# Softmax probabilities normalised ahead of the transposes instead of after the value product

## The reference, cut to what matters

```
N_HEADS = 8; SEQ = 512; CTX_LEN = 256; QK_NOPE_DIM = 64; QK_ROPE_DIM = 32; V_HEAD_DIM = 64
def mla_attend(q_nope, q_rope, k_nope, k_rope, v):
    scale = (QK_NOPE_DIM + QK_ROPE_DIM) ** -0.5
    s = (jnp.einsum('bqhd,bkhd->bhqk', q_nope, k_nope)
         + jnp.einsum('bqhr,bkr->bhqk', q_rope, k_rope))
    pr = jax.nn.softmax(s.astype(jnp.float32) * scale, axis=-1).astype(v.dtype)
    return jnp.einsum('bhqk,bkhd->bqhd', pr, v)
```

## Time and profile before

| what | value |
|---|---|
| median of 3 runs | 885.34 us (885.32 to 887.03) |
| profiled execution, span | 883.6 us |
| busy share over the span: PE, DVE, ACT, POOL | 94 %, 51 %, 43 %, 43 % |
| attention stage, first scores to the end of the last row factors | 138.14 to 246.04 us of the span, 107.9 us |
| busy in that stage: PE, DVE, ACT, POOL | 97.1, 84.0, 75.7, 45.1 us |

### The profile page before, as it was taken

How to read it: one execution, slowest core, us unless ns; L and a number is a source line. 1 busy time by engine, 2 the same in 40 slices (tenths; PEclk the granted TensorE clock), 3 DMA queues, 4 the chain that set the end, 5 groups by cost and what they waited for, 6 DMA issues and landing times.

```text
span 883.6 us, 11658 instructions
## 1 busy us (share of the span) xinstructions
PE 828.0 (94%) x3976; PEld 680.0 (77%) x3976; DVE 451.6 (51%) x560; ACT 376.4 (43%) x580; POOL 376.2 (43%) x191
## 2 busy tenths in 40 slices
PE   5679968999899999999999899999999999999995
PEld 4458856888688888888858798888888888888884
DVE  5853797888723257666423566555555555100014
ACT  6763445778622323222234355444444444211134
POOL 0095352466235445746532335444444444444420
PEclk9979989999999999999999899999999999999998
DMA  8923210011032469856552214333333332322202
GB/s 291 331 64 70 67 48 1 1 48 26 25 90 73 147 194 282 253 176 194 165 166 72 72 29 139 97 97 100 100 100 99 95 95 95 96 96 95 71 1 95
DMA packets 126239, 96.22 MB, mean 109 GB/s; under 512 B 13468, under 2 KB 111033, under 8 KB 126201
## 3 DMA queue, kind: packets, MB, share of 16 engines
q1 hardware_dynamic: 126169, 95.71, 36.0%
q10 hardware_dynamic: 32, 0.01, 0.0%
HBM read 93.60 MB, written 2.10 MB: 108 GB/s over the span
## 4 chain that ended last, share of the span: by engine, by line
PE 77%; DVE 10%; issue 4%; ACT 3%; DMA 3%; POOL 1%; SPq 1%; ACTq 0%; DVEq 0%
PE ps L340 24%; PE ps L342 24%; PE ps L341 24%; DVE small L972 2%; POOL ht L488 1%; PE ps L1357 1%; DVE work L949 1%; DMA xt<-x_dram 1%; PE ps L1346 1%; PE ps L1437 1%; DVE work L953 1%; DVE klo L940 1%; DMA xt<-ctx_dram 1%; DMA raw<-w_in_dram 1%; SPq L223 1%
## 5 line engine op out<-in xcount | busy, mean ns | idle before, releaser
L279 POOL TENSOR_TENSOR wlo<-raw,whi 128x1024 fp32r<-128x1024 f32 (+2 forms) x131 | 306.2, 2342 | 392.2 <-ACT whi L271 391.7
L340 PE MATMUL ps<-hhi,whi 128*128 128x512 f32 (+1 forms) x648 | 251.1, 388 | 8.0 <-DVE hlo L889 4.8
L341 PE MATMUL ps<-hlo,whi 128*128 128x512 f32 (+1 forms) x648 | 249.2, 385 | 0.0
L342 PE MATMUL ps<-hhi,wlo 128*128 128x512 f32 (+1 forms) x648 | 248.9, 384 | 0.0
L271 ACT ACTIVATE whi<-raw 128x1024 fp32r<-128x1024 f32 (+2 forms) x148 | 144.6, 988 | 107.5 <-PE ps L342 88.7
L340 PEld LDWEIGHTS ps<-hhi,whi 128*128 128x128 f32 x648 | 123.5, 191 | 34.0 <-DVE hlo L889 4.8
L342 PEld LDWEIGHTS ps<-hhi,wlo 128*128 128x128 f32 x648 | 123.7, 191 | 23.7
L341 PEld LDWEIGHTS ps<-hlo,whi 128*128 128x128 f32 x648 | 123.7, 191 | 23.5 <-issue 0.5
L1154 DVE SCALAR_TENSOR_TENSOR work<-ps,prm,work 128x511 f32<-128x511 f32 x44 | 33.0, 749 | 76.8 <-ACT work L812 75.9
L1025 DVE SCALAR_TENSOR_TENSOR adacc<-ada,cvec,adacc 128x1024 f32<-128x1024 f32 x28 | 62.2, 2236 | 15.6 <-DMA ada<-w_ada_dram 15.5
L340 PE MATMUL ps<-fhi,whi 128*128 (+1 forms) x176 | 69.2, 393 | 0.1
(11 more groups left out here) (232 smaller groups left out, 1253.1 us busy)
## 6 DMA issues: line engine op xcount, KB each, us to landing
raw<-w_up_dram SPq DMA_DIRECT2D x88, 256.0 KB, 3.1
raw<-w_in_dram SPq DMA_DIRECT2D x66, 256.0 KB, 3.5
ada<-w_ada_dram SPq DMA_DIRECT2D x32, 512.0 KB, 4.7
raw<-w_down_dram SPq DMA_DIRECT2D x44, 256.0 KB, 2.7
raw<-w_ada_dram SPq DMA_DIRECT2D x32, 256.0 KB, 4.7
raw<-w_o_dram SPq DMA_DIRECT2D x16, 256.0 KB, 3.2
xt<-x_dram SPq DMA_DIRECT2D x4, 512.0 KB, 7.0
raw<-w_attn_out_dram SPq DMA_DIRECT2D x8, 256.0 KB, 3.6
```

Of the source, the lines that this page charges most:

```text
L279: ins = (engine or nc.gpsimd).tensor_tensor(out=l, in0=r, in1=h.bitcast(F32), op=ALU.subtract)
L340: pe.matmul(o, l[0], r[0], start=start, stop=False)
L341: pe.matmul(o, l[0], r[1], start=False, stop=False)
L342: return pe.matmul(o, l[1], r[0], start=False, stop=stop)
```

## The change

Each tile of probabilities is divided by its row sums where the queries still lie on the partitions, so that a sum is one scalar per partition. For each g, DVE takes the reciprocal of one column of sums and multiplies the 128 x 768 tile in place (`normalize`). `transposes(g)` waits for that (`p_norm`) instead of for the exponential (`p_exp`). What built the row factors goes: `inverse` on DVE, `diagonals` on POOL, `row_factors` on PE, and the second operation of `output_value` on DVE. POOL's loop also loses its wait for `diag`.

```
-            def inverse(h):
-
-                dve.wait_ge(s("p_exp"), TT * (h + 1))
-                wait(dve, s("diag"), h)
-                nc.vector.reciprocal(inv_sum, exp_sum(TT * h, TT)).then_inc(s("rsum"), 1)
+            def normalize(g):
+
+                dve.wait_ge(s("p_exp"), g + 1)
+                nc.vector.reciprocal(inv_sum(g), exp_sum(g)).then_inc(s("p_inv"), 1)
+                dve.wait_ge(s("p_inv"), g + 1)
+                nc.vector.tensor_scalar(probs(g), probs(g), inv_sum(g), None, ALU.mult).then_inc(s("p_norm"), 1)
 
             def output_value(h):
 ...
-                nc.vector.tensor_tensor(out=work[r, 1, :], in0=ps[0:VDIM, 7, :], in1=work[r, 0, :], op=ALU.add).then_inc(s("o_sum"), 1)
-                dve.wait_ge(s("o_sum"), h + 1)
-                dve.wait_ge(s("r_ps"), h + 1)
-                nc.vector.tensor_tensor(out=work[r, 1, :], in0=ps[r, 6, :], in1=work[r, 1, :], op=ALU.mult).then_inc(s("o_val"), 1)
+                nc.vector.tensor_tensor(out=work[r, 1, :], in0=ps[0:VDIM, 7, :], in1=work[r, 0, :], op=ALU.add).then_inc(s("o_val"), 1)
 
             maxima(0)
             maxima(1)
+            normalize(0)
             for g in range(HEADS * TT):
                 h, t = g // TT, g % TT
                 if g + 2 < HEADS * TT:
                     maxima(g + 2)
-                if t == 2:
-                    inverse(h)
+                if g + 1 < HEADS * TT:
+                    normalize(g + 1)
...
             def transposes(g):
 
-                pe.wait_ge(s("p_exp"), g + 1)
+                pe.wait_ge(s("p_norm"), g + 1)
...
-                pe.wait_ge(s("k_raw"), min(2 * (h // 2) + 4, HEADS))
-                pe.wait_ge(s("diag"), h + 1)
-                pe.matmul(ps[:, 6, :], ones[:], diag, start=True, stop=True).then_inc(s("r_ps"), 1)
...
-            def diagonals(h):
-
-                pool.wait_ge(s("rsum"), h + 1)
-
-                wait(pool, s("r_ps"), h)
-                nc.gpsimd.tensor_tensor(out=diag.rearrange("p (t n) -> p t n", n=P), in0=ident[:].unsqueeze(1).to_broadcast([P, TT, P]),
-                                        in1=inv_sum.unsqueeze(2).to_broadcast([P, TT, P]), op=ALU.mult).then_inc(s("diag"), 1)
```

More of the change, by code:

```diff
@@ L320, in exp_sum, with inv_sum @@
             return small[:, 18 + g % 8:18 + g % 8 + n]
-        inv_sum = small[:, 8:8 + TT]
+        def inv_sum(g):
+            return small[:, 8 + g % TT:9 + g % TT]
         q_rms = small[:, 4:4 + TT]
@@ L328, in neg_bias @@
             return small[:, g % 4:g % 4 + 1]
-        diag = work[:, 5, :]
         G = flat[:, 0:4 * P].rearrange("p (g n) -> p g n", n=P)
@@ L537, in _ @@
             for h in range(HEADS):
-                diagonals(h)
-                pool.wait_ge(s("diag"), h + 1)
                 if h + 2 < HEADS:
@@ L681, in output_part @@
                 act.wait_ge(s("pv_ps"), 2 * h + 2)
-                wait(act, s("o_sum"), h)
+                wait(act, s("o_val"), h)
                 nc.scalar.activation(work[r, 0, :], ps[VDIM:P, 7, :], ACT.Copy).then_inc(s("o_part"), 1)
@@ L1360, in output @@
                     last.then_inc(s("pv_ps"), 1)
-            def row_factors(h):
-                pe.wait_ge(s("k_raw"), min(2 * (h // 2) + 4, HEADS))
-                pe.wait_ge(s("diag"), h + 1)
-                pe.matmul(ps[:, 6, :], ones[:], diag, start=True, stop=True).then_inc(s("r_ps"), 1)
             scores(0)
@@ L1387, in _ @@
                     output(h - 1, 1, 1)
-                    row_factors(h - 1)
                 if new_keys:
@@ L1394, in _ @@
                 output(HEADS - 1, 1, part)
-            row_factors(HEADS - 1)
             for j in range(CT):
```

## The result

The changed kernel takes **895.32 us** (median of four, 894.43 to 897.02) against 885.54 us (885.32 to 887.03) for the kernel before, measured beside it: the ratio is 1.0113 with a 95 % interval of 1.0095 to 1.0131, so 9.8 us slower. The forecast was 894.6 us, with 888.5 to 904.5 as its range. The profiled execution, the slowest of the four, has a span of 895.2 us.

What follows compares the result with a forecast made beforehand. PE led the chain before; DVE was to bound the changed attention stage: 84.0 + 16.3 own work + 7.9 port waits + about 9 idle = 117.2 us, +9.3 on 885.3 gives 894.6 us, range 888.5 to 904.5.

Steps and rivals of the forecast that it cites:

- DVE as the bound: Attention stage: DVE needs 108.2 us, over 92 % busy, about 9 us idle; stage 117.2 against 107.9 us; chance 0.73.
- DVE's own work: Attention stage, per tile: reciprocal 0.20 us plus multiplication 0.51 us, 22.7 us in 32 tiles; less 6.4 us shed, +16.3 us.
- PE's and POOL's savings buy nothing: Attention stage: the 6.9 us PE sheds and POOL's 8.3 us give no time, since DVE sets the pace.
- The port waits: DVE's multiplications wait for POOL at the shared SBUF access: 7.9 us, half-way between 6.1 and 9.8; ends 0 and 16.
- rival 3: Multiplications meet POOL's splits in step with heads 2 to 5: 16 us of waits, about 906 us; chance 0.14 for 901 and above.
- the half-length of a random instruction: A multiplication falling at random into a POOL instruction waits half its length on average; 6.1 us for two-input instructions.
- Whether POOL's one-input split holds the multiplication: Left open for POOL's 2.13 us splits in the attention stage: waits of 9.8 us if it holds, 6.1 us without.
- The middle pair: Two heads mid-stage: 28.0 us of DVE work plus 0.8 idle, 28.8 against 26.61 us; test 28 to 30 us.
- My second way: Cross-check of the stage sum from two heads mid-stage: four pairs of +2.2 us each make +9 us.
- The clock: PE's falls to half speed in the stage: today's one fall kept, each further one costs 0 to 1.7 us.
- rival 1: New DVE work fits its 23.9 us of idle time, PE's 6.9 us come off: 878.4 us at best; chance 0.06.

Runs made afterwards that it cites:

- the control: Second measurement of the unaltered changed kernel, beside the run with matmuls added: 896.92 us, ratio 1.0130 to the kernel before.
- the run with added matmuls: Changed kernel with four unread matmuls of 512 columns where the row factors stood, for seven of eight heads: ratio 1.0102 to the kernel before.
- the addition only: Kernel before with the per-tile reciprocal and multiplication added, row factors kept, so both divisions are done: ratio 1.0192 to the kernel before.
- the one-input product: Changed kernel with the 128 x 1 product of maximum and scale written as tensor_scalar: ratio 1.0019, measured again 1.0026, to the kernel before.
- mended versions: Changed kernel with the product as tensor_scalar (1.0019, again 1.0026), with the reciprocal behind the next maximum (1.0024), or with both (1.0026).
- delayed splits: Changed kernel with POOL's four weight splits in the stage each held back until a given multiplication is done: ratio 1.0054 to the kernel before.
- light splits: Changed kernel with POOL's four weight splits in the stage cut from 1024 to 128 columns: ratio 1.0069 to the kernel before.
- the removal run: Changed kernel without its reciprocals and multiplications, so the division by row sums is left out: ratio 0.9911 to the kernel before, -7.2 us.
- 256 columns: Changed kernel with the multiplication over 256 of the 768 columns, the rest unscaled: ratio 1.0044 to the kernel before.
- the reciprocal moved: Changed kernel with a tile's reciprocal moved behind the next maximum, ahead of the two-input product: ratio 1.0024 to the kernel before.

## Why the prediction was right, step by step

**DVE as the bound: right.** Its need was put at 108.2 us, and it was 108.25 and 108.11. The edge of it came out softer than I wrote: 90.1 % and 91.5 % busy in the stage, where over 92 % was to be seen, and 11.9 and 10.0 us idle instead of 9. PE had idle time before the transposes as forecast, but less busy time only in the control (92.5 for 97.1 us). The multiplication's shortest, 0.62 us, is as forecast; its mean is 0.92 where I had near 0.8. In the chain of waits inside the stage DVE's lines L963, L991, L965, L972, L994 and L931 have 50 %, and over the whole span its share rose from 10 % to 13 %, as the page of the changed kernel has it:

```profile
PE 76%; DVE 13%; issue 4%; ACT 2%; DMA 2%; POOL 1%; SPq 0%; ACTq 0%; DVEq 0%
```

**DVE's own work: right.** From the reciprocal to the multiplication 194.68 - 194.50 = 0.18 us, from there to the next start 195.22 - 194.68 = 0.54, in all 0.72 against 0.71.

**PE's and POOL's savings buy nothing: right for PE**, by the run with added matmuls. In the kernel before, the removal as a whole is worth 7.2 us; that includes 4.8 us less on DVE, so it is no price of PE alone. POOL's saving was not tested by itself.

**The port waits: right in sum, wrong in kind.** I had 7.9 us for a random meeting, half-way between two readings. The multiplications alone waited 9.8. Beside them, two terms that I left out nearly cancel: the product took 1.8 us more (9.2 for 7.4), and the key split on DVE 2.7 us less (3.8 for 6.5). The sum is 8.9 us. But the mechanism is that of rival 3: waits at fixed places of heads 2 to 5, four of 2.1 us. I had given it 16 us and a chance of 0.14. It had the right instructions and not the right block: it saw the multiplication meeting the query split and the weight split at its start, 1.28 + 2.39 us. In fact the product takes the first part of that wait and the multiplication the second. The step that failed is the half-length of a random instruction. It should have been read from the order of the instructions on both engines, which says what stands on DVE when a POOL instruction ends. So the forecast of 894.6 us came as close as it did partly by luck. Nor is the waiting product the only way into such a meeting: with the addition only, one of four long multiplications (2.68 us at 233.34) followed a product that took its undisturbed 0.16 us.

**Whether POOL's one-input split holds the multiplication, which no row before showed:** in part. At 184.98 it took 1.12 us and ended at 186.10, 0.41 us after L513 had ended (185.69). But the changed kernel itself has one that was not held, DVE first and POOL second:

```profile
162.34 0.62 DVE L972 TENSOR_SCALAR prob<-prob,small 128x768 f32<-128x768 f32 x1
161.40 2.24 POOL L513 TENSOR_SCALAR khi<-work 64x768 fp32r<-64x768 f32 x1
```

and with the one-input product one was held for a short while and ended well before the split:

```profile
190.17 0.82 DVE L972 TENSOR_SCALAR prob<-prob,small 128x768 f32<-128x768 f32 x1
189.75 2.13 POOL L513 TENSOR_SCALAR khi<-work 64x768 fp32r<-64x768 f32 x1
```

Over all the traces it goes by the moment at which the multiplication starts, counted from the start of the split. Those that began 0.34 to 0.53 us after it ended 1.24 us after it (7 cases), those at 0.76 to 1.10 took 0.61 or 0.62 us (15 cases), and those at 1.41 to 1.70 were held to the end. So this split holds the multiplication near its start and near its end, and lets it pass between. In the changed kernel the one-input splits cost the multiplications 1.3 us, and the four weight splits 8.5. The Trainium skill ("SBUF — State Buffer", section "SBUF: two separate sides") has the shared port pair as an exclusive lock that whichever side starts first keeps for the whole instruction. For the weight splits this case agrees in both directions: 2.72 us behind a weight split, and a weight split of 2.58 us behind a multiplication. For the one-input split it does not: 0.62 us at 162.34. The 9.8 us that the prediction had by that page is also what the multiplications waited, but by chance: that figure too came from random meetings, and it had the one-input splits at 3.7 us of it.

**The middle pair:** 28.8 us were worked out, 28 to 30 named as the test; it took 30.97, in the control 222.74 - 191.37 = 31.37. My second way had spread the waits over four pairs, and they lie in the two middle ones. With the one-input product the pair takes 214.80 - 188.28 = 26.52 us, no more than the 26.61 of before.

**The clock:** one stretch of the stage was granted half speed before, two in the control, three in the other execution. These two executions of the same kernel differ by 2.0 us in the stage at equal DVE work, in line with the 0 to 1.7 us for each fall. No run isolates it.

**Where the time went, then.** DVE got 24 us of busy time, of which some 15 are work and 9 waits. The idle time of the stage took up 12 to 14 us. With a large part of the waits gone the change costs 2 us (three mended versions, +1.8 to +2.8). So the loss is not, as the sum suggested, mostly the multiplication's length; the work nearly fitted, and the waits came on top at close to full price, because by then DVE was the bound (delayed splits: 5.7 us less on DVE and 6.2 us in time; light splits: 7.4 and 5.8). Whether rival 1 would come true with no waits at all is open: the mended versions still hold 3 to 6 us of them. Why DVE keeps 9 to 11 us of idle time even then was not taken apart, and no mended version beat the kernel before.

## What to carry to other kernels

Before giving DVE a long operation of one fp32 tensor from SBUF to SBUF, write down what POOL has queued at that place, and look for a short DVE instruction between a shared wait and the long one: here a reciprocal of 0.15 us in that place went with a wait of 2.1 us, four times, and the versions without that order were 9 to 10 us faster. A small product of two SBUF tensors next to a busy POOL should be written with a scalar per partition, or placed directly ahead of the long operation. Where no long operation stood behind it, in the kernel before, the same rewriting bought nothing that could be measured. Work taken from PE counts only where PE sets the pace; here 6.9 us of matmuls were worth nothing once DVE did.

## What the runs showed of the hardware

- A 128 x 1 product of two SBUF tensors on DVE takes 0.16 us alone and up to 1.99 us (in the removal run) beside POOL. Where it had to wait for a POOL operation of two tensors it ended 0.01 to 0.03 us behind it, in all such cases in the traces of ten runs.
- POOL's operation of one tensor (L513, 2.13 us) holds the same product only in its first part: the product ended 0.83 to 0.84 us after that operation's start if it had to wait (0.29 us at 164.92 before, 0.63 at 161.60 after), and took 0.16 us if it came later, as at 180.73 in the earlier trace rows.
- The same operation holds a multiplication of 128 x 768 by a scalar at both of its ends and not between, as told above: it ended 1.24 us after the operation's start, or undisturbed, or 2.53 to 2.55 us after that start, 0.40 to 0.43 us behind the operation's end.
- Behind a POOL operation of two tensors a multiplication that had to wait ended 0.40 to 0.42 us after it (0.14 or 0.15 us with 256 columns), which is less than its own 0.62 us (0.35 us).
- The product with a scalar operand took 213 to 217 ns in all 32 cases, whatever POOL did (194 to 217 ns in the four runs that have it).
- A POOL operation that comes second is lengthened too, by less in these traces, where it meets shorter instructions: 2.39 to 2.58 us for the weight split, 1.28 to 1.62 us for the query split with the reciprocal moved.
